# The moving columns of a product are streamed in pieces of 32 or 34, taken by turns from two places

## What is computed

```python
def swiglu(h, w_in, w_out):                       # w_in 1024 x 5632, w_out 2816 x 1024
    gate, up = jnp.split(h @ w_in, 2, axis=-1)
    return (jax.nn.silu(gate) * up) @ w_out
...
    proj = h @ w_in                               # gla 1024 x 3072, dsa 1024 x 1864
...
    proj = hn @ w_in                              # retention 1024 x 6144
...
    return rmsnorm_2(h, final_g)[:, PAD + N_META:]
```

## Time and profile before

| | us |
|---|---|
| median of the two runs shown | 1376.2 |
| the two runs | 1376.01 and 1376.38 |
| span of the profiled execution, first to last instruction | 1374.3 |
| PE busy | 1366.9 (99% of the span) |
| weight loads (PEld), beside the matmuls | 1300.8 (95%) |
| DVE busy | 1000.4 (73%) |
| ACT busy | 702.7 (51%) |
| POOL busy | 296.2 (22%) |

### The profile page before, as it was taken

How to read it: one execution, slowest core, us unless ns; L and a number is a source line. 1 busy time by engine, 2 the same in 40 slices (tenths; PEclk the granted TensorE clock), 3 DMA queues, 4 the chain that set the end, 5 groups by cost and what they waited for, 6 DMA issues and landing times.

```text
span 1374.3 us, 24685 instructions
## 1 busy us (share of the span) xinstructions
PE 1366.9 (99%) x9888; PEld 1300.8 (95%) x9888; DVE 1000.4 (73%) x1580; ACT 702.7 (51%) x1154; POOL 296.2 (22%) x288
## 2 busy tenths in 40 slices
PE   9999999999999999999999999999999999999998
PEld 9999999999999888899999999999999999988886
DVE  6688766656986988788676875766657886798843
ACT  7465544444746555544334563544435465655543
POOL 1136000023153000032255644000022623120000
PEclk9999999999999999999999999999999999999999
DMA  8334565665443755556443355555554554466552
GB/s 275 123 123 157 186 190 182 187 187 164 138 145 103 230 182 187 169 178 197 141 152 131 123 184 161 179 183 181 163 179 131 178 149 150 140 213 187 190 191 77
DMA packets 220457, 229.72 MB, mean 167 GB/s; under 512 B 13664, under 2 KB 207704, under 8 KB 220344
## 3 DMA queue, kind: packets, MB, share of 16 engines
q1 hardware_dynamic: 219232, 226.24, 51.2%
q10 hardware_dynamic: 1112, 1.90, 0.6%
HBM read 226.80 MB, written 1.33 MB: 166 GB/s over the span
## 4 chain that ended last, share of the span: by engine, by line
PE 98%; DVE 1%; DMA 0%; issue 0%; ACT 0%; ACTq 0%; DVEq 0%
PE ps L558 27%; PE ps L556 20%; PE ps L557 20%; PE ps L553 14%; PE ps L1085 1%; PE ps L1084 1%; PE ps L1083 1%; PE ps L869 1%; PE ps L946 1%; PE ps L616 1%; PE ps L618 1%; PE ps L617 1%; PE ps L750 1%; PE ps L936 1%; PE ps L738 0%; PE ps L837 0%
## 5 line engine op out<-in xcount | busy, mean ns | idle before, releaser
L1125 ACT ACTIVATE uh<-raw 128x1024 fp32r<-128x1024 f32 (+4 forms) x452 | 446.7, 998 | 455.4 <-PE ps L558 391.0
L1694 DVE TENSOR_TENSOR ul<-raw,uh 128x1024 fp32r<-128x1024 f32 (+3 forms) x448 | 528.9, 1188 | 137.6 <-PE ps L558 89.0
L558 PE MATMUL ps<-xx,ul 128*128 128x272 f32 (+1 forms) x2136 | 610.7, 286 | 0.0
L556 PE MATMUL ps<-xx,uh 128*128 128x272 f32 (+1 forms) x1448 | 424.7, 293 | 0.0
L557 PE MATMUL ps<-xx,uh 128*128 128x272 f32 (+1 forms) x1448 | 415.8, 287 | 0.0
L558 PEld LDWEIGHTS ps<-xx,ul 128*128 128x128 f32 x2136 | 401.7, 188 | 0.0
L556 PEld LDWEIGHTS ps<-xx,uh 128*128 128x128 f32 x1448 | 272.6, 188 | 4.0 <-issue 1.7
L557 PEld LDWEIGHTS ps<-xx,uh 128*128 128x128 f32 x1448 | 272.9, 188 | 0.8
L558 PE MATMUL ps<-aa,ul 128*128 128x272 f32 (+1 forms) x920 | 262.6, 285 | 0.0
L553 PE MATMUL ps<-xx,uh 128*128 128x512 f32 x704 | 247.4, 394 | 0.0
L556 PE MATMUL ps<-aa,uh 128*128 128x272 f32 (+1 forms) x788 | 228.7, 290 | 0.0
(11 more groups left out here) (327 smaller groups left out, 1609.7 us busy)
## 6 DMA issues: line engine op xcount, KB each, us to landing
raw<-in_ffn_w SPq DMA_DIRECT2D x62, 1024.0 KB, 5.3
raw<-in_ffn_w_in SPq DMA_DIRECT2D x44, 1024.0 KB, 5.1
raw<-in_ret_w_in SPq DMA_DIRECT2D x24, 1024.0 KB, 5.1
raw<-in_ffn_w_out SPq DMA_DIRECT2D x16, 1024.0 KB, 5.3
raw<-in_gla_w_in SPq DMA_DIRECT2D x11, 1024.0 KB, 5.1
raw<-in_ret_w_o SPq DMA_DIRECT2D x8, 1024.0 KB, 5.1
raw<-in_dsa_w_in SPq DMA_DIRECT2D x7, 1024.0 KB, 5.6
raw<-in_ffn_w_out SPq DMA_DIRECT2D x8, 768.0 KB, 5.0
```

Source lines behind the costliest of these rows:

```text
L556: e.matmul(ps[:, 0:n1 - n0], hi[:, k, :], x.hi[:, k0 + j, n0:n1], start=first and j == 0, stop=False)
L558: i = e.matmul(ps[:, 0:n1 - n0], lo[:, k, :], x.hi[:, k0 + j, n0:n1], start=False, stop=last and j == len(ks) - 1)
L1125: i = e.activation(unit_hi(u)[:, :, cols], a, ACT.Copy)
L1694: i = e.tensor_tensor(unit_lo(u)[:, :, cols], a, unit_hi(u)[:, :, cols].bitcast(F32), ALU.subtract)
```

## The change

Two helpers split the columns of an operand. `halves` cuts a row of n columns into eight pieces of n/8 (34 of 272, 32 of 256) and takes them by turns from the first and the second half of the row: columns 0 to 33, 136 to 169, 34 to 67, 170 to 203 and so on. `parts_by_turns` does it for line 553's two parts: 32 columns of the high part, the same 32 of the low part, the next 32 of the high part, in sixteen pieces. The result is written by the same pattern, so each column lands where it did, and whoever reads PSUM finds what it found. Number, order, waits and weights of the instructions stay; `rows`, `columns`, the matmuls of the packed units (lines 537 and 539) and the fp32 products are as before.

```diff
+            def halves(a):
+
+                n = a.shape[-1] // 8
+                return a.rearrange("p (q s c) -> p s q c", q=2, c=n)
+
+            def parts_by_turns(a):
+
+                return a.rearrange("p a (s c) -> p s a c", c=32)
...
+                    to, xh_k = halves(ps[:, 0:n1 - n0]), halves(x.hi[:, k0 + j, n0:n1])
                     if pair:
-                        e.matmul(ps.rearrange("p (a n) -> p a n", a=2), hi[:, k, :], x.pair[:, :, k0 + j, n0:n1],
-                                 start=first and j == 0, stop=False)
+                        e.matmul(parts_by_turns(ps.rearrange("p (a n) -> p a n", a=2)), hi[:, k, :],
+                                 parts_by_turns(x.pair[:, :, k0 + j, n0:n1]), start=first and j == 0, stop=False)
                     else:
-                        e.matmul(ps[:, 0:n1 - n0], hi[:, k, :], x.hi[:, k0 + j, n0:n1], start=first and j == 0, stop=False)
-                        e.matmul(ps[:, 0:n1 - n0], hi[:, k, :], x.lo[:, k0 + j, n0:n1], start=False, stop=False)
-                    i = e.matmul(ps[:, 0:n1 - n0], lo[:, k, :], x.hi[:, k0 + j, n0:n1], start=False,
-                                 stop=last and j == len(ks) - 1)
+                        e.matmul(to, hi[:, k, :], xh_k, start=first and j == 0, stop=False)
+                        e.matmul(to, hi[:, k, :], halves(x.lo[:, k0 + j, n0:n1]), start=False, stop=False)
+                    i = e.matmul(to, lo[:, k, :], xh_k, start=False, stop=last and j == len(ks) - 1)
```

## The result

The changed kernel takes 1412.8 us (median of two runs, 1412.78 and 1412.81) against 1376.2 us: a ratio of 1.0265, with a 95% interval of 1.0249 to 1.0282. It is slower by 36.6 us. No change was forecast.

A forecast was written before the change was run, and what follows sets the result against it. PE, busy 99% at full clock, was taken as the bound, 1128 us of it in edited lines. New jumps added 0 to the 1374.3 us span; with 1.9 us around it, 1376.2 us, range 1315 to 1421.

The forecast's parts named there:

- the price of a jump in the read: Moving-operand reads of the edited matmuls: each new jump costs zero, as line 553's one jump showed; 0 us.
- 0.7 ns a jump: Upper bound for a jump in the read, from line 553's distances; over all 64,512 new jumps +45.2 us, 1421.
- The misaligned piece: Pieces of 34 in 272-column matmuls, half starting at an odd multiple of 8 bytes: unpriced, bound inside that of a jump.
- Rival 2: All new jumps, in misaligned reads of 34 or in writes: at least a cycle each, 1403 to 1421 us; chance 0.16.
- The zero for the write: PSUM result writes of the edited matmuls: new jumps cost zero, though no row of the trace shows one.
- rival 3: PSUM writes: each jump costs like a new matmul start, 4.0 ns, +258 us, 1634 us; chance 0.08.
- Rival 1: Edited matmuls: two streams by turns take away the excess per column, half of it, 1342 us (1309 to 1352); chance 0.36.
- the excess over one column a cycle: Edited matmuls: each column costs 0.0275 ns, some 6.6%, more than a cycle; all the change can gain.
- the 67.5 us: The excess per column summed over the 2.454 million columns of the edited lines; the most the change could gain.
- The sum of the edited lines: Lines 558, 556, 557 and 553 on PE: matmul counts times start-to-start distances make 1128.0 us, as the chain has it.

The follow-up runs named there:

- on_grid_34: Changed kernel with only the 272-column reads by turns, eight pieces of 34, each begun on a multiple of 16 bytes, 36 columns apart; writes straight: 1422.6 us.
- pieces_2: Changed kernel with only 272-column matmuls by turns from two halves, in 136 pieces of 2 columns, read and write; other widths straight: 1671.7 us.
- gaps_34: Changed kernel with only 272-column reads cut, eight pieces of 34 begun on multiples of 16 bytes, in rising order without turns; writes straight: 1408.1 us.
- step_16_all: Changed kernel with 272- and 256-column products in groups of 4, every fourth group in four rounds, read and write; pairs straight: 1353.7 us, ratio 0.9838.
- step_68: Changed kernel with only 272-column matmuls reordered: four groups of 4 standing 68 columns apart, then back 200 columns to the next four: 1372.3 us.

## Why the prediction was wrong

- **The step that failed is the price of a jump in the read.** "I take zero for both kinds, because it is what the only row with a jump shows". The row was right: line 553's one jump goes from a whole group to a whole group, once in 512 columns. It was no sample of what the change makes, seven or fifteen jumps in every matmul. With whole groups throughout they cost 1.5 ns (256 columns) and 5.2 ns (a pair), 6.7 us of the 36.6. The bound that stood beside it, 0.7 ns a jump, had the size: 36.6 us over 64,512 are 0.57. That bound is why 1412.8 us still lies within the range. The prediction's last sentence had named this way to fail: that a lone jump says nothing of many.
- **The misaligned piece was set inside the bound of a jump** ("its bound is inside that of a jump"), with no term of its own. It was the larger part: 30.2 us stand in the 272-column matmuls, whose pieces of 34 are 8.5 groups of 16 bytes. Pieces of 34 without turns lose 6.3 ns; whole groups by turns lose 0.3 (four pieces of 68) and 1.5 (eight of 32, in a row of 256). By these, an estimate, 3.6 to 4.8 of the 5.1 ns are the half groups' part. What "half of them start at an odd multiple of 8 bytes" missed is that the other half end there: beginning all of them on the grid took nothing away (on_grid_34, 8.9 ns), and a piece of 34 touches nine groups wherever it begins. The rows alone don't show groups of 16 bytes; with them, which the runs gave, the price can be estimated from the earlier trace rows: a straight stream spends 4 x 0.444 = 1.8 ns on a group, and a row in pieces of 34 touches 72 instead of 68, which makes 7.1 ns and 42 us, a high end with a reason behind it. Measured were 0.7 (pieces_2, with its write: 49.9 ns for 68 more) to 2.2 ns (on_grid_34, with its turns: 8.9 for 4) for a touch more, and 1.5 with neither (gaps_34: 6.1 for 4).
- **Rival 2 was the right one** in place and size: the read of a misaligned piece of 34, 1403 to 1421. Its price, a cycle for every jump, was not the mechanism: 33 jumps between whole groups cost less than 7 with half ones, so that the size fits so well is luck. I had given it 0.16.
- **The zero for the write was right**, and rival 3 fell with it: writes in pieces of 34 and 32 cost 0.0 us, and writes in pieces of 4 stand in kernels faster than before. Of the two statements of the Trainium skill, the one of "PSUM — Partial Sum Buffer", Specifications (TRN2), that any non-contiguous pattern slows matmuls significantly, doesn't agree with that; the one of "Advanced Engine Details and Errata", Memory Cachelines, that every two consecutive elements should be contiguous, does, as far as pieces of 32 and 34 can show. The same section of the Trainium skill gives SBUF cachelines of 16 bytes, the size of the groups found here, and says that at least two hits on one are needed to absorb the memory's latency; pieces of 2 columns have just two, and took 175.6 ns for 125.7, read and write together.
- **Rival 1**: the excess over one column a cycle can be reduced by the order, but not by this order. step_16_all took back 5928 x 2.7 + 1616 x 4.6 = 23.4 us by its distances (22.2 by its time), a third of the 67.5 us.
- **The sum of the edited lines** (1128 us), that nothing else bounds, and that unedited matmuls stay at 117.7 and 231.4 held.

What stays open: why two places by turns cost and four in turn (step_68) don't, why the turns add 2.8 ns to pieces begun on the grid and take 1.2 from those of the changed kernel (6.3 without, 5.1 with), why steps of 64 bytes win while steps of 128 lose, and whether pieces shorter than 32 cost or win in the read or in the write. The runs give the prices and no mechanism.

## What to carry to other kernels

Where a float32r stream is the bound, cut a moving operand at multiples of four fp32 columns only, and price a pattern first by the 16-byte groups that it touches: one more cost 0.7 to 2.2 ns here, around the 1.8 ns that four columns take. The order of the groups moved the price by up to 5 ns beside that, and how the result is cut cost nothing at pieces of 32 and 34. A row of the trace that shows one jump prices one jump: before taking it for many, look at what is special about it, here that it fell on a group's edge. And the order within a row is worth a try even where PE seems at its limit: the same columns taken 64 bytes apart, in read and write, took 2% (272 columns) and 4% (256) less than in sequence, while 128 bytes apart they took 2% more.

## What the runs showed of the hardware that I had not expected

- The excess per column of a float32r product depends on the order of the columns (read and write in the same order here, and the write had proved free at pieces of 32 and 34): 125.7 ns straight, 123.0 in steps of 64 bytes, 130.7 by turns from two halves, with the same columns and the same 68 groups; for 256 columns 118.1, 113.5 and, with steps of 128 bytes, 120.5.
- Reading each group twice (pieces of two columns) makes 175.6 of 125.7 ns, not twice as much: (175.6 - 4.0)/136 = 1.26 ns a touch, against (125.7 - 4.0)/68 = 1.79 for a whole group in sequence. The write is in pieces of two there as well, so the part of the reads may be smaller.
- An accumulating write to PSUM by turns in pieces of 32 and 34 costs 0.0 us over 8380 matmuls. Writes in pieces of four columns were run only together with reads of the same order; the pair of them was faster than straight (step_16_all), so in that order they can cost little.
